# The gate stage of two expert layers: activations laid out experts-inside, one gate product a group, and one-hot columns made with two tensor operands

## What is computed

```
q = (h @ peer_q).reshape(B, S, PEER_HEADS, 2, PEER_HALF)
scores = jnp.einsum('bshpd,hpkd->bshpk', q, peer_keys)
s, i = lax.top_k(scores, PEER_TOPK)
...
top_s, sel = lax.top_k(cand_s, PEER_TOPK)
idx = jnp.take_along_axis(cand_i, sel, axis=-1)
gate = jax.nn.softmax(top_s.astype(jnp.float32), axis=-1)
...
u_sel = jnp.take(peer_u, ix, axis=0)
v_sel = jnp.take(peer_v, ix, axis=0)
act = jax.nn.gelu(jnp.einsum('td,ted->te', hx, u_sel), approximate=False)
return jnp.einsum('te,ted->td', gx * act, v_sel)
```

## Time and profile before

| | us |
|---|---|
| median of 3 runs | 4019.97 (4017.22 to 4025.73) |
| the profiled execution | 4015.35 |
| its span | 4013.6 |
| start of the first and of the last gate matmul | 562.9 and 3645.7 |
| PE busy in the span | 3871.0 (96%) |
| DVE busy | 3028.2 (75%) |
| POOL busy | 1070.5 (27%) |

### The profile page before, as it was taken

How to read it: one execution, slowest core, us unless ns; L and a number is a source line. 1 busy time by engine, 2 the same in 40 slices (tenths; PEclk the granted TensorE clock), 3 DMA queues, 4 the chain that set the end, 5 groups by cost and what they waited for, 6 DMA issues and landing times.

```text
span 4013.6 us, 76989 instructions
## 1 busy us (share of the span) xinstructions
PE 3871.0 (96%) x27054; PEld 3418.3 (85%) x27054; DVE 3028.2 (75%) x5829; ACT 2268.4 (57%) x4081; POOL 1070.5 (27%) x666
## 2 busy tenths in 40 slices
PE   6999999999999999999998999999998999999999
PEld 6898888888889888888888988888887788888887
DVE  6768889777566888976766787987775678797555
ACT  4256577545534656854556566865454556685554
POOL 0104458000010345810000244741000034482000
PEclk9999999999999999999998999999998999999999
DMA  8345553878514555387853555458882255534554
GB/s 286 129 142 187 185 167 130 280 255 284 169 50 137 173 188 173 127 274 243 288 173 116 175 182 192 137 198 294 285 285 108 75 179 183 192 125 165 192 192 155
DMA packets 203691, 749.53 MB, mean 187 GB/s; under 512 B 22704, under 2 KB 23856, under 8 KB 202192
## 3 DMA queue, kind: packets, MB, share of 16 engines
q1 hardware_dynamic: 178416, 646.51, 48.2%
q0 software_dynamic: 25056, 100.15, 7.8%
HBM read 745.52 MB, written 1.05 MB: 186 GB/s over the span
## 4 chain that ended last, share of the span: by engine, by line
PE 83%; POOL 7%; ACT 4%; DVE 4%; issue 1%; DMA 1%; POOLq 0%; SPq 0%; ACTq 0%; DVEq 0%
PE ps L2162 16%; PE ps L2632 12%; PE ps L2639 12%; PE ps L2635 12%; PE ps L2170 9%; POOL t_lo L658 4%; PE ps L2134 4%; PE ps L2135 3%; PE ps L2141 3%; ACT t_hi L736 3%; PE ps L2311 2%; PE ps L2566 2%; PE ps L2567 2%; POOL oh L651 1%; PE ps L2575 1%; POOL t_lo L636 1%
## 5 line engine op out<-in xcount | busy, mean ns | idle before, releaser
L736 ACT CAST t_hi<-raw 128x1024 fp32r<-128x1024 f32 x1180 | 1241.6, 1053 | 965.8 <-PE ps L2639 689.5
L1245 DVE TENSOR_TENSOR t_lo<-raw,t_hi 128x1024 fp32r<-128x1024 f32 x880 | 1077.0, 1225 | 590.9 <-ACT t_hi L736 570.8
L2162 PE MATMUL ps<-h_both,t_hi 128*128 128x512 f32 x3040 | 762.2, 393 | 0.0
L2162 PEld LDWEIGHTS ps<-h_both,t_hi 128*128 128x128 f32 x3040 | 546.6, 189 | 97.7
L636 POOL TENSOR_TENSOR t_lo<-raw,t_hi 128x1024 fp32r<-128x1024 f32 x176 | 450.7, 2561 | 625.5 <-ACT t_hi L736 625.5
L2632 PE MATMUL ps<-t_hi,h_both 128*128 128x512 f32 x2048 | 548.0, 389 | 5.4 <-DVE h_both L2023 5.4
L2639 PE MATMUL ps<-t_lo,h_both 128*128 128x512 f32 x2048 | 547.4, 389 | 0.0
L2635 PE MATMUL ps<-t_hi,h_both 128*128 128x512 f32 x2048 | 547.3, 389 | 0.0
L2134 PE MATMUL ps<-h_both,t_hi 128*128 128x256 f32 x1792 | 470.6, 299 | 24.2 <-DVE h_both L1419 11.8
L2632 PEld LDWEIGHTS ps<-t_hi,h_both 128*128 128x128 f32 x2048 | 384.0, 188 | 85.3 <-issue 6.1
L2635 PEld LDWEIGHTS ps<-t_hi,h_both 128*128 128x128 f32 x2048 | 384.5, 188 | 79.9
(11 more groups left out here) (325 smaller groups left out, 5178.6 us busy)
## 6 DMA issues: line engine op xcount, KB each, us to landing
raw<-u_tiles SPq DMA_DIRECT2D x512, 512.0 KB, 3.5
raw<-v_tiles SPq DMA_DIRECT2D x512, 512.0 KB, 4.2
raw<-w_tiles SPq DMA_DIRECT2D x188, 512.0 KB, 3.5
oh<-w_tiles POOLq DMA_DIRECT2D x160, 512.0 KB, 4.8
arena<-w_tiles SPq DMA_DIRECT2D x16, 512.0 KB, 4.0
arena<-keys_t POOLq DMA_DIRECT2D x4, 1024.0 KB, 6.8
arena<-mla_w POOLq DMA_DIRECT2D x1, 4096.0 KB, 14.5
arena<-lora POOLq DMA_DIRECT2D x2, 1280.0 KB, 8.8
```

The lines of the kernel that those rows point to most:

```text
L736: act.copy(t_hi[:, j % SPL, :], raw[:, j % RAW, :]).then_inc(hi_done, 1)
L1245: tts(t_lo[:, j % SPL, :], raw[:, j % RAW, :], t_hi[:, j % SPL, :].bitcast(F32), ALU.subtract).then_inc(lo_done, 1)
L2162: mm(ps[:, j % 2, :], hi[:, c, :], h_both[:, c, :, :].rearrange("p a t -> p (a t)"), start=(c == 0), stop=False)
```

## The change

Three edits. The arena's block becomes (b, q, t, e): the token comes before the expert-tile, so the 16 entries of a block and quad are still one run, but a tile's 256 tokens lie 4 elements apart. The matmul of a token writes its 128 gates as 32 runs of 4 (b, with t fixed, e inside), so a PSUM bank has the same order as the arena, and one instruction over both banks multiplies all 1024 entries of a group. And DVE's columns, before `tensor_scalar` with two scalars (compare with the column number, multiply with the weight), become `scalar_tensor_tensor`, whose weight is a tensor operand, broadcast.

```diff
-        act_at = arena[:, :].rearrange("p (b q e t) -> p b q e t", b=KEYS // EB, e=EB, t=4)
+        act_at = arena[:, :].rearrange("p (b q t e) -> p b q t e", b=KEYS // EB, e=EB, t=4)
...
-                return act_at[:, k // EB, :, k % EB, :]
-            return act_at[:, bass.ds(i + k // EB, 1), :, k % EB, :].rearrange("p b q t -> p (b q) t")
+                return act_at[:, k // EB, :, :, k % EB]
+            return act_at[:, bass.ds(i + k // EB, 1), :, :, k % EB].rearrange("p b q t -> p (b q) t")
...
-                        ts(hot_cols[m % 2][:, q, :], iota, sel[:, 1, t:t + 1], sel[:, 2, t:t + 1], ALU.is_equal, ALU.mult)
+                        stt(hot_cols[m % 2][:, q, :], iota, sel[:, 1, t:t + 1], sel[:, 2, t:t + 1].broadcast_to([P, P]),
+                            ALU.is_equal, ALU.mult)
...
-                    for q in range(2):
-                        view = act_at[:, :, 2 * m + q, :, :]
-                        ins = tts(view, ps[:, GATE_BANKS[m % 2] + q, :].rearrange("p (t b e) -> p b e t", t=4, e=EB),
-                                  view, ALU.mult)
-                    ins.then_inc(gated, 1)
+                    view = act_quads[:, :, 2 * m:2 * m + 2, :].rearrange("p b q x -> p q b x")
+                    bank = GATE_BANKS[m % 2]
+                    tts(view, ps[:, bank:bank + 2, :].rearrange("p q (b x) -> p q b x", x=4 * EB),
+                        view, ALU.mult).then_inc(gated, 1)
...
-                            o = ps[:, GATE_BANKS[b] + q // 4, (q % 4) * P:(q % 4 + 1) * P]
+                            o = ps[:, GATE_BANKS[b] + q // 4, :].rearrange("p (b t e) -> p b t e", t=4, e=EB)[:, :, q % 4, :]
```

## The result

| | us |
|---|---|
| changed kernel, median | 4091.82 (4086.87 to 4093.03, 4 runs) |
| kernel before, median | 4018.59 (4014.0 to 4025.73, 4 runs) |
| ratio | 1.0176, 95% interval 1.0161 to 1.019 |
| span of the profiled execution, before and after | 4013.6 and 4090.8 |

A forecast was written before the change was run, and what follows sets the result against it. TensorE bounds the u and v stretches; GpSimd's lower half and DVE's columns, excluding each other, bound the gate stages. Columns +11 and product -0.3 made +11 us: 4026, or 4031 against the runs' median; range 4014 to 4052.

The forecast's parts named there:

- The ring of lower half, columns and L1965: Gate stage: GpSimd's lower half and DVE's columns and row one-hots exclude each other, setting 4.25 us a group.
- 31 computed: Gate stages: gain of 31 us if the new columns are not held by GpSimd's lower half, 3989 us; 12%.
- the next ring's 4.01 us: Gate stage: lower half, GpSimd's column, TensorE's matmuls and products, and the cast could run at 4.01 us a group.
- Part 1: Gate product: one of 1024 elements for two of 512; covered by the wait for the lower half, -0.3 us in all.
- Part 2: DVE's new columns in the gate stage: still held, 0.09 us more a group, +11 us in all.
- the bound of 16: Upper bound on the new columns' cost in the gate stage, given as 0 to +16 us.
- Part 3: Columns beside GpSimd's fills before the gate stage: no longer stopped, taken as 0, at most -2.6 us.
- Part 4: Activations' layout, one element in each 16 bytes of SBUF: taken as 0, open to +40 us over four layers.
- the upper end: Activations' layout: twice the element cost, +0.26 us for each DVE instruction, up to +40 us over four layers.
- Part 5: Gate matmuls writing PSUM in runs of four: taken as 0, between no change and double time.
- the slack of 0.49 us: Gate stage: spare time over two groups on the path through TensorE and the cast, to hide +0.4 of slower matmul writes.
- The layout's rival: Layout and PSUM writes cost their upper ends: +11 and some +10 to +50 us, 4040 to 4080, 4060 middle; 13%.

The follow-up runs named there:

- run 7: Kernel before with column numbers copied to PSUM for DVE's row and column one-hots, scalar_tensor_tensor columns and one gate product: 3990.39 us, ratio 0.9909.
- run 5: Kernel before with one gate product a group, reading across both PSUM banks; arena and matmul writes as before: ratio 1.0005.
- run 1: Kernel before with the new scalar_tensor_tensor columns alone, old layout and two gate products: 4034.07 us, ratio 1.0043.
- run 2: Kernel before with the new arena layout alone, old columns, two gate products, matmuls writing 128 columns together: 4099.32 us, ratio 1.0191.
- run 9: Changed kernel with the old tensor_scalar columns put back: 4088.77 us, ratio 1.0146 to the kernel before.
- run 10: Kernel before with GpSimd's column of a group moved ahead of its lower half, nothing else: 4024.0 us, ratio 0.9988.
- run 3: Kernel before with one gate product, arena unchanged, gate matmuls writing single PSUM columns 4 apart: 4068.83 us, ratio 1.0129.
- run 4: Changed kernel with one added wait, GpSimd's first lower half starting only after DVE's second row one-hots: 4073.5 us, ratio 1.0142 to the kernel before.

## Why the prediction was wrong, point by point

- **What bounds the gate stage: right.** The ring of lower half, columns and L1965 was read off the rows, and run 7 took it apart: the gain (32 us in the gate stages, 31 computed) and the next ring's 4.01 us came out.
- **Part 1, the product: right.** Nothing while covered (run 5, ratio 1.0005).
- **Part 2, the columns: right, 0.09 for 0.123.** The first column's longer reading is +0.07, as taken. The others start 0.27, 0.29 and 0.26 us apart, not 0.263. The 0.03 for the middle one lies where GpSimd's column runs; beside it the forecast had seen only a full hold or none. +15 us instead of +11 (run 1), inside the bound of 16.
- **Part 3, the fills: wrong in size.** "0, at most -2.6 us" was right for the kernel before. But the hold is not bounded by the length of one fill. With the layout it was 2.65 to 4.5 us, 2 to 5 us of each u stretch with what the granted clock adds (runs 2 and 9), which the new columns give back. It is no matter of the layout alone: with the u stretch and columns of before, columns stood 3.7 us or more in one layer of run 5 and in two of run 10. The execution that the forecast was read from had met it in no layer.
- **Part 4, the layout: the step that failed.** "I take 0: the nearest row is today's L1990, which reads PSUM". It was the wrong memory, and the next sentence said so; for SBUF no row stood against the upper end, so the value had to lie nearer to it. The upper end itself was good (+0.26 an instruction against +0.21 measured). DVE's busy time in the u stretch grew by 31 us where the upper end had 25: 20 for the sum, and 10 for selection steps with two inputs in SBUF (L1863, L1871, L1874), which now ran into GpSimd's lower halves for longer. What it costs could not be read from the mean: the 8.3 us a layer fall on some 17 of 95 tiles, which take 3.1 to 3.8 us from one tile's first L2170 to the next one's where the median is 2.8. At these tiles DVE has its long selection steps and a lower half together. The waits of layer 0's u stretch show it, the kernel before and then the changed one:

```profile
PEld ps L2170 <- DVE t_lo L1245: 0.8, 1, 0.8
...
PEld ps L2170 <- DVE t_lo L1245: 9.5, 21, 1.2
```

  In the v stretch the cover held (+1.0 us in all).
- **Part 5, TensorE's writes: right for the change, but the cover behind it wasn't there.** Runs of four cost nothing (0.058 us a matmul). But a step would have cost nearly double (run 3), and the slack of 0.49 us that was to hide it did not: the first eight matmuls were counted as covered, and with TensorE itself at 4.6 us a group there is no cover. The rule of the Trainium skill (Advanced Engine Details and Errata, section Memory Cachelines: a pattern in PSUM that is not contiguous slows matmuls) agrees with the trace at steps of 8 and 16 bytes; for runs of 16 bytes it doesn't hold, and the measurement decides.
- **Missing altogether: the second rhythm, +16.5 us.** The prediction took the order of L1965 and L658 from the steady state of before and never asked what sets it. It is the first turn. Before, DVE's four columns began 0.19 us ahead of the stage's first gate matmul and were over when L658 came 1.44 us behind it. With the layout they begin later, after a late L1245, while L658 still comes at 1.44. In layers 1 to 3 it just holds: L1965 and L658 start within 0.02 us of each other. In layer 0 DVE stands 0.34 us more ahead of the columns, the fourth falls behind L658's start (577.71), and the order turns. Layer 0 and then layer 1:

```profile
577.02 3.31 DVE L1975 SCALAR_TENSOR_TENSOR oh<-cst,sel 128x128 f32<-128x128 f32 x4 [0.34 <-issue]
...
1624.16 1.14 DVE L1975 SCALAR_TENSOR_TENSOR oh<-cst,sel 128x128 f32<-128x128 f32 x4
1625.22 1.22 DVE L1965 TENSOR_TENSOR acc<-cst,sel 128x1024 f16<-128x1024 f32 x1
...
1625.21 3.48 POOL L658 TENSOR_TENSOR t_lo<-raw,t_hi 128x1024 fp32r<-128x1024 f32 x1 [6.40 <-ACT t_hi L736]
```

  Of the 48 gate stages in the twelve traces the slow rhythm stands in three, layer 0 of the changed kernel and of runs 2 and 9, and these are the three in which the fourth column starts behind L658. Where layer 0's 0.34 us come from is open. The code waits there for the last GELU (L1173), but that had ended 0.45 us before the columns began, and equally early in layers 1 to 3, which have no such gap; the profile names no releaser ("issue"). Run 2 has the rhythm without the new columns, run 4 removes it without touching them.
- **The range.** The layout's rival stood at 13% with 4060 in the middle. With the layout at its upper end as the likeliest case the sum would have been 4031 + 33 = 4064; the second rhythm and the 5 us more of columns make 4085 of it, and the mixing parts' own variation the rest.

Not settled: what the new columns are worth inside the changed kernel, +15 us in the gate stage against what they give back ahead of it (18 us by run 2's u stretches, 13 by run 9's), since the executions of either run differ among themselves by more than that difference; and what makes layer 0's 0.34 us.

## What to carry to other kernels

A layout is paid for at every place that touches it: here one product instruction a group (128 in all) was bought with 0.2 to 0.25 us on each of over 2000 others, when a stepped read of PSUM would have done it for nothing. Where two engines exclude each other, list what each instruction reads and writes in SBUF and take an operand out of it; that was worth 37 us, and removing the longest visible wait first was worth nearly nothing. And where two engines that exclude each other run in a loop, look at the first turn, since it can lock in an order for the whole loop: here a start 0.34 us later went with 16.5 us.

## What the runs showed of the hardware

- SBUF, float32, 256 elements a partition at a step of 16 bytes: DVE 0.631 us against 0.424, ACT 0.628 against 0.373; on ACT a write alone (L1179) costs as much more as a read and a write (L1173, 0.687 against 0.421). Runs of two: 0.439 and 0.433.
- TensorE writing 128 float32 columns to PSUM: 0.109 us a matmul at steps of 8 and of 16 bytes, 0.058 together and in runs of four.
- DVE reading PSUM at a step of 512 bytes: 1024 elements in 1.225 us, and 1.225 in whole runs too.
- A tensor_scalar of DVE from SBUF to SBUF stood 4.46 us behind GpSimd's fills, which follow each other without a gap; scalar_tensor_tensor at the same place took 0.34. Columns that start equally against the fills stood 1.05 us in three layers and 3.74 in the fourth (run 5).
